# Second block's attention: the order of differential and grouped pairs within a query tile

## What is computed

```python
def _diff_attention(dq, dk, dv, lam):
    s = jnp.einsum('bqhjd,bkhjd->bhjqk', dq, dk).astype(jnp.float32) * ATTN_SCALE
    p = jax.nn.softmax(s, axis=-1)
    a = (p[:, :, 0] - lam * p[:, :, 1]).astype(dv.dtype)
    return jnp.einsum('bhqk,bkhe->bqhe', a, dv)

def _gqa_attention(gq, gk, gv):
    s = jnp.einsum('bqhgd,bkhd->bhgqk', gq, gk).astype(jnp.float32) * ATTN_SCALE
    p = jax.nn.softmax(s, axis=-1).astype(gv.dtype)
    return jnp.einsum('bhgqk,bkhd->bqhgd', p, gv)
```

## Time and profile before

| | us |
|---|---|
| median of 3 runs | 3932.5 (3932.43 to 3933.34) |
| the profiled execution | 3933.81 |
| its span in the trace | 3931.9 |
| attention, first layer, first score to last product with values | 1346.9 to 1521.8 |
| attention, second layer | 2985.8 to 3127.2 |

### The profile page before, as it was taken

How to read it: one execution, slowest core, us unless ns; L and a number is a source line. 1 busy time by engine, 2 the same in 40 slices (tenths; PEclk the granted TensorE clock), 3 DMA queues, 4 the chain that set the end, 5 groups by cost and what they waited for, 6 DMA issues and landing times. The chain is left out here.

```text
span 3931.9 us, 47902 instructions
## 1 busy us (share of the span) xinstructions
PE 3729.5 (95%) x18308; PEld 2555.2 (65%) x18308; DVE 1867.9 (48%) x3512; ACT 832.4 (21%) x1688; POOL 1031.1 (26%) x888
## 2 busy tenths in 40 slices
PE   7988789999999999999998999999999999989998
PEld 6776545555565586555554555555887767778887
DVE  4466323222412376886545666656125655143445
ACT  3125211111201264111213000002124611220001
POOL 2331100000023202132332222232142034443443
PEclk9999899999999999999999999999999999999999
DMA  5410599999411100222221222221120022212221
GB/s 213 187 71 1 220 351 395 394 395 398 195 59 54 38 1 17 93 89 77 102 79 54 108 107 107 107 87 53 49 76 23 12 75 81 81 65 97 86 86 54
DMA packets 72302, 475.13 MB, mean 121 GB/s; under 512 B 8272, under 2 KB 9680, under 8 KB 18960
## 3 DMA queue, kind: packets, MB, share of 16 engines
q1 hardware_dynamic: 68864, 461.35, 31.3%
q0 software_dynamic: 2640, 8.65, 0.8%
q10 hardware_dynamic: 576, 2.10, 0.1%
HBM read 467.87 MB, written 4.19 MB: 120 GB/s over the span
## 5 line engine op out<-in xcount | busy, mean ns | idle before, releaser
L1030 PE MATMUL ps<-projected,weight_ring 128*128 128x384 f32 (+1 forms) x672 | 245.8, 521 | 0.0
L3598 PE MATMUL ps<-projected,weight_ring 128*128 128x384 f32 (+1 forms) x768 | 223.0, 434 | 1.2 <-DVE mlp_u L3797 0.7
L2478 DVE SCALAR_TENSOR_TENSOR sb_x_all<-ps,sb_modulation_ada,sb_x_all 128x512 f32<-128x512 f32 x144 | 106.5, 750 | 244.6 <-PE ps L2303 215.0
L1030 PEld LDWEIGHTS ps<-projected,weight_ring 128*128 128x128 f32 x672 | 127.7, 190 | 106.1 <-issue 45.9
L3598 PEld LDWEIGHTS ps<-projected,weight_ring 128*128 128x128 f32 x768 | 144.8, 190 | 62.5 <-issue 3.0
L3598 PE MATMUL ps<-projected,mlp_weight_sums 128*128 128x384 f32 x480 | 165.8, 488 | 0.0
L1398 DVE TENSOR_REDUCE attention_shift<-ps 128x1 f32<-128x768 f32 (+1 forms) x160 | 130.9, 846 | 59.6 <-PE ps L1268 59.5
L2138 POOL DMA_INDIRECT h<-tokens,own_tokens x31 | 31.1, 1004 | 487.2 <-PE ps L2274 416.1
L3001 DVE SCALAR_TENSOR_TENSOR projected<-projected,sb_vectors 128x497 f32<-128x497 f32 (+26 forms) x270 | 157.9, 650 | 1.6
L3598 PE MATMUL ps<-h2b,weight_ring 128*128 128x384 f32 (+1 forms) x512 | 151.2, 439 | 6.5 <-ACT h2b L943 6.5
L2861 PE MATMUL ps<-projected,gate_sums 128*128 128x384 f32 (+1 forms) x512 | 151.1, 439 | 3.8 <-POOL gate_sums L3141 3.8
(11 more groups left out here) (670 smaller groups left out, 7697.6 us busy)
## 6 DMA issues: line engine op xcount, KB each, us to landing
weight_ring<-w_stream SPq DMA_DIRECT2D x217, 1024.0 KB, 5.0
expert_weights<-w_moe SPq DMA_DIRECT2D x125, 1024.0 KB, 23.0
weight_ring<-w_moe SPq DMA_DIRECT2D x40, 1024.0 KB, 23.3
h2b<-w_moe SPq DMA_DIRECT2D x33, 1024.0 KB, 23.1
weight_ring<-w_stream SPq DMA_DIRECT2D x16, 512.0 KB, 3.7
weight_ring<-w_stream SPq DMA_DIRECT2D x16, 384.0 KB, 3.2
sb_x_all<-xT SPq DMA_DIRECT2D x4, 768.0 KB, 7.2
tokens<-h_tokens ACTq DMA_DIRECT2D x4, 512.0 KB, 9.3
```

Of the source, the lines that this page charges most:

```text
L1030: ins = nc.tensor.matmul(core.ps[:, 2 * slot + half, 0:n], w_of(k), h_of(k)[:, a:a + n], start=(first and k == 0), stop=(last and k == chu ...
L2478: v.scalar_tensor_tensor(core.x[:, k, NCTX:T], ps[:, bank, :], core.mods["ada"][:, 40 + k, 1:2], core.x[:, k, NCTX:T], ALU.mult, ALU.add). ...
L3598: ins = nc.tensor.matmul(acc, wq[:, k, :], bq[:, k, :], start=(first and k == 0), stop=(last and k == 3), skip_group_check=True)
```

## The change

The second `for c in range(4):` goes. The grouped pair of index c now follows directly on the differential pair of index c, so that a query tile's list is D G D G D G D G where it was D D D D G G G G. Nothing else is edited: the pipeline, its waits and the buffers by parity of p are as before. Because buffers go by parity, all D pairs now use the even set and all G pairs the odd set.

```diff
                             "diff": True, "keys": keys, "spans": [(0, keys)],
                             "v": lambda i, c=c: dv[:, i, c * P:(c + 1) * P],
                             "out": pr[:, DQ + c, q]})
-                    for c in range(4):
                         pairs.append({
                             "maps": [(pr[r:r + HD, GQ + c, q], pr[r:r + HD, GK + c // 2, :])
                                      for r in (0, HD)],
```

## The result

| | us |
|---|---|
| before, median of 6 runs | 3932.92 (3926.15 to 3938.41) |
| after, median of 6 runs | 3949.82 (3946.26 to 3953.94) |
| ratio | 1.0039, 95% interval 1.0027 to 1.0051 |
| profiled execution after, its span | 3949.95, 3948.0 |

The alternated order is slower by 0.39%. The forecast was 3947.3, or 1.0038 of before.

The account below looks back on a forecast made before the run. PE was taken to bound both attention phases. 13.1 us for the 768-key tiles, 1.0 for the 256-key tiles and 0.7 for the ends gave +14.8, so 3947.3 us (1.0038 of before), range 3940 to 3953.

Parts of the forecast that it names:

- heavy step: 768-key tiles, DVE's G copies and D mix in one step: four per tile, transposes 6.49 after T0, wait 0.44 us.
- light step: 768-key tiles, step behind the D pair's transposes: DVE waits for PE, next T0 at 8.86 us per two pairs.
- first rival: 768-key tiles: DVE's slack in the step with little work removes the waits; 3932 to 3934 us, chance 7%.
- Scaling or mix: DVE's scaling or mix holds PE before the D pair's transposes; which one counts was said not to matter for the sum.
- point of 5.86: 768-key tiles: the mix must end before 5.86 us after T0, 0.44 less than the rows show, for no wait.
- ACT: 768-key tiles, ACT's copy of the D pair before T0: 0.28 us of cover left, costed at nothing.
- second rival: An exponential slips before ACT's D pair copy, T0 late by 0.62 in about 32 turns: 3967 us, chance 7%.
- 256-key tiles: Two small tiles, T0 waiting for ACT's copy: 4.19 us per two pairs, +1.0 us for both tiles.
- third rival: PE's clock falls in the attention stretches; 3974 us if a tenth ran at 1.2 GHz, chance 3%.
- The ends: Start and drain of each layer's attention phase: 0.35 us per layer within bounds 0 and 1.2, +0.7 in all.
- The sum: Whole kernel: +14.8 us from the 768-key tiles, 256-key tiles and phase ends, to 3947.3 us.

Follow-up runs that it names:

- copy_twice: Against the alternated kernel, DVE does its 384-column copy after T1 of a G pair twice, once into an unread spare buffer; 3964.28 us in one run.
- layer1_only: Alternated order in the second layer alone, the first layer as in the kernel before; 3940.38 us in one run.
- scale_early: Against the alternated kernel, in steps with a mix DVE scales pair p - 3 ahead of the reciprocal and ratio of pair p - 1; 3948.97 us.
- three variants: Whole copy after T1 of a G pair on ACT, in orders D D G G, D D D D G G G G, D G D G: 3929.84, 3931.72, 3935.54 us.
- the three on the two waits: Alternated kernel with the scaling moved ahead, the mix cut to 256 of 768 keys, or both: 3948.97, 3953.77 and 3940.19 us.
- t1_act: Against the alternated kernel, the whole copy after T1 of a G pair (896 columns) goes to ACT; 3935.54 us, 1.0004 of the kernel before.

## Why the prediction was right, point by point

- **The heavy step, four times per tile.** Right, with its mechanism and its price. 6.49 was forecast from T0 to the transposes, 6.50 is in the trace. Removing 0.46 us of DVE's work from the step gave the time back, adding 0.46 cost exactly that. This is shown, not only argued.
- **The light step.** Right: `gv` 0.91 behind the transposes, T0 1.46 behind `gv`, 8.86 forecast and 8.87 found. DVE waits there, and its slack does not reach the heavy step. The first rival, in which it does, falls.
- **Scaling or mix.** The prediction left it open as without weight for the sum, and for the sum that held. It took the 0.19 from the end of the mix to the transposes for the distance at which the one releases the other. The runs show 0.05 for that (above), so the scaling ends last, by 0.13. The point of 5.86 for the end of the mix, at which its first rival was to decide, rests on the same 0.19. By the scaling, its start would have to come at 6.05 - 1.40 = 4.65, where the rows have 5.10. That is 0.45 less, and the prediction asked for 0.44, so nothing changes for the rival.
- **ACT.** Right, with its cover intact. In the profile after, ACT's copy of a D pair ends at 3086.20 (start 3085.28) and T0 starts at 3086.63. The second rival falls in the 768-key tiles. At the start of the phase ACT is the wait, as was said.
- **256-key tiles.** Right: 4.19 per two pairs (T0 at 1364.17 and 1368.36). ACT's copy of the D pair ends at 1364.03 (1363.54 + 0.49), 0.14 before T0, so T0 does wait for it there.
- **The clock.** 1.00 in the steady stretches, so as a cost of the new waits the third rival falls. By the rule of the Trainium skill that the prediction names, which gives no size for its short idle times, the clock could have gone up and down; waits of 0.44 in 8.87 us did not do that here, nor did the longer ones of `copy_twice` (0.90 in 9.33 us, clock 1.00 from 1384 to 1516 and from 3013 to 3130). Outside the steady stretches `copy_twice` did lose clock, as the next point says.
- **The ends.** This is the term that was too small, 0.7 for both layers. In the second layer the phase takes 7.2 more in `layer1_only`, of which the tiles explain 4 x 1.67 = 6.7, so 0.5 is left. In the first layer it grew from 174.9 to 184.8: the tiles give 6.7 and the small tiles 1.0, and 2.2 is left. Most of it is in the drain, below, where products ran at half clock: 1.2 us in the one product and 0.4 in the T0 behind it. Without these 1.6 the ends come to about 0.6 and 0.5 us, where 0.35 was forecast for each. The half clock does not follow from the wait of 1.74 alone: the second layer's drain in the same profile has the same wait and its product takes 1.53, and a wait of 1.86 in `scale_early` kept the full clock in both layers. With a wait of 2.20, in `copy_twice`, both drains fell to about half (the product took 2.73 and 2.83). The wait for the mix in the drain comes with the alternation, since the order before ends in G pairs only. When it costs the clock stays open.
- **The sum.** The two phases together grew by 20.7 us in the profiled pair (first layer 9.9, second 10.8), the whole execution by 16.1. The half clock at the start of the second layer's phase makes about 3.6 of the 20.7. Outside the phases the profile after is 4.6 shorter, with nothing edited there. The runs of one and the same kernel before lie between 3926 and 3943 us, so one pair of profiles can't tell a cause for that, and I have none. The medians, 16.9 apart, carry the same scatter. That they meet the forecast of 14.8 within 2.1 us is partly luck. The steps of 6.50 and 8.87 us, which were forecast row by row, are not.

The drain of the first layer in the profile after, PE alone:

```profile
1521.32 1.50 PE L1306 MATMUL ps<-attention_prob_t,dv 128*128 128x128 f32 x12
1524.56 0.87 PE L1286 MATMUL ps<-sb_constants,attention_prob 128*128 128x128 f32 x6 [1.74 <-DVE attention_prob L1417]
...
1525.47 2.72 PE L1306 MATMUL ps<-attention_prob_t,gv 128*64 128x128 f32 x24
```

With no scores left to fill the time, PE waits 1.74 for the last mix, and the product behind it takes 2.72 in place of 1.53. The granted clock over the next stretch was 0.60:

```profile
1525.00:1528.00 3.00, 3.00 (x29) 2.62 (x27) 0.00 (x0) 0.92 (x1) 0.00 (x0) 0.60 0.02 5
```

## What to carry to other kernels

In a pipeline that is written out in steps, add up each engine's work per step and not per phase: if two kinds of item meet in one step, an engine that is busy for 71% on average can be the one that ends last there, and the slack of the next step does not help if its chain starts from the slow engine's result. Before an order is changed, look for the one place in the present trace where the new neighbourhood already occurs; its rows price the change. When a wait is shortened and nothing moves, look for a second one that ended almost with it, and at whether the edit has moved that one too. To tell which of two waits held an engine, compare the distance from each to the start of the engine's work with the same distance at a place where only that one can have held it.

## What the runs showed of the hardware

What a kind of product costs PE depends a little on what follows it: the product with `dv` takes 1.43 us up to the following scores and 1.34 up to a following T0, and the spread tile takes 0.10 or 0.11 up to `dv` and 0.20 up to `gv`. For `gv` no such difference shows (1.46 or 1.47 either way). These rows do not say why. The differences between three variants (33.30, 33.54, 33.76 us per tile) are nearly all made of such terms, with the waits of 0.05.

Where nothing but a DVE result holds PE, PE starts about 0.05 us after the DVE instruction ends: 0.05 behind the mix of `scale_early`, 0.06 in the drain, and 0.05 behind the scaling in `copy_twice`.

The granted clock at the start of the second layer's phase differs between executions. It was at half rate nearly throughout from 3002 to 3008 in the profile after (two last rows), where before it fell for a shorter time (columns as above, kernel after):

```profile
2999.00:3002.00 3.00, 2.74 (x16) 1.97 (x17) 2.26 (x5) 2.08 (x6) 0.40 (x1) 0.70 0.00 0
3002.00:3005.00 3.00, 1.90 (x10) 1.53 (x9) 1.35 (x3) 1.80 (x3) 0.40 (x1) 0.50 0.00 0
3005.00:3008.00 3.00, 3.00 (x15) 2.09 (x14) 0.43 (x1) 1.48 (x3) 0.00 (x0) 0.50 0.00 0
```

PE had waited 1.84 and 1.10 us just ahead of and in this stretch. Six other kernels whose second layer alternates (the three on the two waits, `t1_act`, `layer1_only` and `copy_twice`) have the same wait of 1.10 for the copy at the start of the phase, and their T0 behind it takes 0.84 or 0.85, where it takes 1.51 in the profile after. The mean clock from 2984 to 3014 is 0.94 in all six, as before has it, and 0.77 in the profile after, though the phase starts at different points of that stretch. What decides which it will be stays open.
